# A hybrid decoder step: first two tiles by chunks, passage reordered with early clears, three query tiles from un-normalised sums

## The chip, the cores and the metric

One core of a Trainium2 chip runs one launch. The metric is the device time of the launch in microseconds (us); for several executions, the median. TensorE (PE) does the matmuls, VectorE (DVE), ScalarE (ACT) and GpSimd (POOL) the elementwise work, and SyncE (SP) issues most DMAs.

## What is computed

288 tokens of width 1024 (a prompt of 256 and eight samples of 4) go through one decoder layer:

```python
z = x @ w_in                                  # queries, keys, values, gates of two mixers
o_A = stick_breaking(...)                     # 8 heads x 64; the samples have 256 cached rows each
o_B = g0*compressed + g1*selected + g2*window # 8 heads, 2 groups, masked softmax with ALiBi
m = concat(rms(o_A) * g_A, rms(o_B) * g_B) @ w_out
h = (a - mean(a)) * rsqrt(var(a) + eps) * g + b      # a = alpha * x + m
q = h @ w_q                                   # 8 heads x 2 x 128
s = q . sub_keys; top-16 of each half, top-16 of the 16 x 16 sums -> 16 experts and weights a head
y = LayerNorm(alpha * h + sum weight * gelu(u_e . h) * v_e)
```

All is float32; keys, values and windows are returned too.

## The kernel before

**Tiles.** A weight tile is 128 x 1024 (512 KB). SP loads it into one of four ring slots; ACT rounds it to `w_hi` (L1225), DVE subtracts to get `w_lo` (L1606, issued in turn by `low_next`). An operand x is split in the same way. `project` (L650 to L652) then makes hi.hi, hi.lo and lo.hi for eight 128-column blocks into one PSUM bank: 24 products a tile.

**Stages.** 22 tiles of w_in (evacuated by ACT, counted by `z_sb`), the gates, the attention passage, 8 tiles of w_out, LayerNorm, 16 tiles of w_q with `pair_scores` after each pair of query tiles, then 128 tiles of the expert table u with routing on DVE, and 128 of v.

**Start.** SP loads w_in tile 0 in halves and x in quarters, ACT and SP share the x loads. 13 idle products (L674) run meanwhile. DVE forms `x_lo` (L1640) for each of eight blocks; tile 1 follows tile 0.

**Passage.** Each engine has its order written out by hand. PE: stick-breaking sums and the compression of the caches, then the samples' scores: 32 products with the cached keys `ks` (L782) and 8 with the new keys (L785) for each of two halves, each half released by eight `ks` page loads (`k_in`); ss_qk is raised at their end. Then values of the prompt (L722), transposes (L793, `ss_t`), `ns_scores` on selected and window keys (L802, L804), `ckT` (L820), compressed values (L828), compressed scores of samples (L834) and prompt (L842), `np_scores` (L858, L861), the samples' reverse sums (L924 to L928, `ss_tri`), and eight units `np_turn` (L873) / `np_values` (L894) with `ns_values` (L947) at the end. DVE: `lss` (L1731), `spb` (L1738), `ssc`, `sc_`, `np_max(0)`, `np_max(1)` (L1792, L1793), `nc_scale` (L1766), `np_scale`. ACT: `np_exp` (L1337), logarithms (L1317).

**Queues.** SP: w_in, 16 `ks` pages of 256 KB (L451), winkv, two writes of kv_out, three w_out tiles behind `ss_tri`, then eight writes of zeros of 1 MB each into `g_dram` (L462, 512-byte rows, called clears), the other w_out tiles, w_q. POOL: 16 `nsk` loads of 128 KB (L563), the `vs` loads (L567, L573) and, ahead of the units, a memset of the zeros (L569).

**LayerNorm.** `residual` (L1899) adds m to alpha x; squares on ACT; sums over features by products with ones (L1024 to L1030). While mean and deviation are made, PE runs `filling(22)` (L1020). DVE subtracts the mean (`center`, L1932) and multiplies by g and the deviation (`stretch`, L1936); ACT adds b and rounds to `h_hi` (L1435); DVE makes `h_lo` (L1941). The first three query tiles are taken together by blocks (L1059 to L1072) as the rows of h come.

Of the kernel before, what the change touches and what calls it, by code (L numbers as in the profile page):

```python
# [24 lines left out]
D = 1024  # L25
# [3 lines left out]
NB = 8  # L29
TS = 4  # L30
T = TP + NB * TS
DT = TP
SLOTS = 32
# [101 lines left out]
def trunk(nc, xT, w_in, w_gate, w_out, w_q, keysT, uT, v, u_rows, w1, pe_cmp, w2, vecs, ln2_rows, cache_sb, cache_nsa,  # L135
# [3 lines left out]
    with ctx:  # L139
# [66 lines left out]
        spb = at("spb", [128, 2, 2, PAST + 32], o + VA * T)  # L206
# [7 lines left out]
        lrow = at("lrow", [128, T], o + 7 * T)  # L214
        o += ZT * T
# [36 lines left out]
        lss = at("lss", [128, 768], at_ring + 1536)  # L252
        sc_ = at("sc_", [128, 8, 2, 32], at_cmp + 4096)
# [15 lines left out]
        w_hi = [at(f"w_hi{q}", [128, D], where, F32R) for q, where in enumerate(E + P + [at_a + KD * T + 2560])]  # L269
        w_lo = [at(f"w_lo{q}", [128, D], where + D, F32R) for q, where in enumerate(E + P + [at_a + KD * T + 2560])]  # L270
# [6 lines left out]
        qT = at("qT", [128, 4, T], r0)  # L277
# [95 lines left out]
        rm_add, ln_s, ln_q, ln_mu, ln_mu2 = map(sem, ("rm_add", "ln_s", "ln_q", "ln_mu", "ln_mu2"))  # L373
# [58 lines left out]
        def _(sp):  # L432
# [6 lines left out]
            sp.dma_start(ring[:, 0, 0:512], w_in[0][:, 0:512]).then_inc(x_in[0], 16)  # L439
            sp.dma_start(ring[:, 0, 512:D], w_in[0][:, 512:D]).then_inc(full[0], 16)  # L440
            for q in range(2, 4):
                sp.dma_start(xTs[:, 2 * q:2 * q + 2, :], xT[:, 2 * q:2 * q + 2, :]).then_inc(x_in[q], 16)
            for n in range(1, N_IN):
# [95 lines left out]
        def _(pool):  # L539
# [7 lines left out]
            pool.dma_start(wg[:, :, :], w_gate).then_inc(small_in, 16)  # L547
            nc.gpsimd.memset(qs_diag[:, :, :], 0.0)
# [20 lines left out]
            nc.gpsimd.memset(spread_out[:, :], 0.0)  # L569
# [68 lines left out]
        def _(pe):  # L638
# [34 lines left out]
            for _ in range(13):  # L673
                mm(ps[:, 7, :], idle_bits[:, 0:64].bitcast(BF16), idle_bits[:, :].bitcast(BF16), start=True, stop=True)  # L674

            x_parts, o_parts, h_parts = (x_hi, x_lo), (o_hi, o_lo), (h_hi, h_lo)
            with pe.Fori(0, 5) as i:
                for r in range(4):
                    pe.wait_ge(z_sb, 4 * i + r + 1)
                    project(r, x_parts, r, halves(i, r), x_low=None if r else x_l)  # L680
# [93 lines left out]

            pe.wait_ge(q_ready, 1)
# [21 lines left out]
            ins.then_inc(ss_t, 1)  # L797

            def ns_scores(br, keys_of):
# [3 lines left out]
                for w in range(2):  # L803
                    mm(ps[:, (3, 0)[br] + w, PAST:PAST + 32], qbd_b[:, 4 * w:4 * w + 4, :],  # L804
                       zT[:, (SK, WK)[br], TP:T], start=True, stop=True)
# [3 lines left out]
            ns_scores(0, lambda b: nsk[:, 2 * b:2 * b + 2, 0:128])  # L809
            for w in range(2):  # L810
                mm(ps[:, 3, 320 + w * 24:344 + w * 24], k("selrow", 32)[:, w * 128:(w + 1) * 128], gnat[0:32, 2, :],
                   start=True, stop=True)
            pe.wait_ge(win_in, 16)
            pe.wait_ge(ss_new, 1)
            ns_scores(1, lambda b: winkv[:, b, 0:PAST])

            hd = hdn[:, :, :].rearrange("p j (s g n) -> p j s g n", g=2, n=NC_)
            pe.wait_ge(ch_sb, 1)
            for g in range(2):
# [1565 lines left out]
```

## Time and profile before

| | us |
|---|---|
| three runs | 1017.07, 1020.25, 1020.06 |
| their median | 1020.06 |
| the profiled execution | 1017.82 |
| its span, first to last instruction | 1016.1 |
| PE busy in the span | 1005.5 |
| DVE busy | 825.8 |
| ACT busy | 547.3 |
| POOL busy | 363.1 |

The page gives shares over the whole span; the change touches the first 14 us, 65 to 170 us and 195 to 220 us, so those are read as timelines. A timeline row shows when an instruction (or a run of like ones, xcount) starts, how long it lasts, and in brackets how long its engine had been idle and what released it. The products of PE are pipelined: a row's time may overlap the next.

### The profile page before, as it was taken

Reading aid. Unit: us, or ns where it says so; the run is one execution under the profiler, and the core shown is the slowest. Engines: PE = TensorE matmul, PEld = TensorE weight load, DVE = VectorE, ACT = ScalarE, POOL = GpSimd, SP = SyncE. Lnnn points to the kernel's source line nnn. Section 1 sums busy time; section 2 is a strip of 40 time slices with the busy share of each in tenths; the row PEclk is TensorE's granted clock in tenths of the full one; section 3 lists DMA queues with packets and bytes.
Section 4 is the critical chain, followed back from the end, with each engine's and each line's share of the span. In section 5 each row is a group of like instructions: output and inputs, shape, how many; then the busy total and the mean of one; then the engine's idle time right before and its main releaser. Section 6 shows DMA issues by size and latency. Waiting matters only on the chain.

```text
span 1016.1 us, 21539 instructions
## 1 busy us (share of the span) xinstructions
PE 1005.5 (99%) x6603; PEld 891.5 (88%) x6603; DVE 825.8 (81%) x1834; ACT 547.3 (54%) x1040; POOL 363.1 (36%) x274
## 2 busy tenths in 40 slices
PE   9999999999999999999999999999999999999997
PEld 7997748999999999998888999988888888888875
DVE  5346577777899897889998699888888889999887
ACT  5436576553545444455556655455555555555553
POOL 0242300000088888888887884011111111111000
PEclk9999999999999999999999999999999999999999
DMA  8758889444588999998999967778888999899763
GB/s 286 261 213 273 277 282 315 151 134 143 189 217 206 240 334 308 318 346 269 277 262 293 236 133 191 246 251 276 311 297 301 310 322 319 306 306 300 261 219 124
DMA packets 124880, 261.75 MB, mean 258 GB/s; under 512 B 29168, under 2 KB 70144, under 8 KB 123520
## 3 DMA queue, kind: packets, MB, share of 16 engines
q1 hardware_dynamic: 91728, 204.60, 60.0%
q0 software_dynamic: 32816, 56.01, 20.7%
q10 hardware_dynamic: 288, 0.59, 0.2%
q8 instruction: 20, 0.33, 0.1%
q14 instruction: 28, 0.23, 0.1%
HBM read 236.83 MB, written 26.38 MB: 259 GB/s over the span
## 4 chain that ended last, share of the span: by engine, by line
PE 96%; DVE 2%; ACT 1%; DMA 0%; issue 0%; DVEq 0%; SPq 0%; ACTq 0%
PE ps L650 12%; PE ps L651 12%; PE ps L652 12%; PE ps L1168 11%; PE ps L1169 11%; PE ps L1170 11%; PE ps L1113 8%; PE ps L1115 4%; PE ps L1145 3%; PE ps L742 2%; PE ps L1039 1%; PE ps L894 1%; PE ps L873 1%; PE ps L861 1%; DVE w_lo L1606 1%; DMA ring<-in_w_in_dram 0%
## 5 line engine op out<-in xcount | busy, mean ns | idle before, releaser
L1606 DVE TENSOR_TENSOR w_lo<-ring,w_hi 128x512 fp32r<-128x512 f32 (+1 forms) x440 | 384.5, 878 | 109.1 <-ACT w_hi L1225 91.4
L1225 ACT CAST w_hi<-ring 128x512 fp32r<-128x512 f32 (+1 forms) x437 | 338.1, 774 | 75.1 <-PE ps L1170 54.4
L587 POOL DMA_INDIRECT gates<-spread_out,spread_at x128 | 241.8, 1889 | 128.7 <-DVE spread_out L2067 82.3
L650 PE MATMUL ps<-h_both,w_hi 128*128 128x256 f32 (+1 forms) x776 | 225.3, 290 | 0.3 <-issue 0.3
L651 PE MATMUL ps<-h_both,w_hi 128*128 128x256 f32 (+1 forms) x776 | 221.2, 285 | 0.0
L652 PE MATMUL ps<-h_both,w_lo 128*128 128x256 f32 (+1 forms) x776 | 220.1, 284 | 0.0
L1168 PE MATMUL ps<-w_hi,y_hi 128*128 128x512 f32 x496 | 193.2, 390 | 0.0
L1169 PE MATMUL ps<-w_hi,y_lo 128*128 128x512 f32 x496 | 193.0, 389 | 0.0
L1170 PE MATMUL ps<-w_lo,y_hi 128*128 128x512 f32 x496 | 193.0, 389 | 0.0
L650 PEld LDWEIGHTS ps<-h_both,w_hi 128*128 128x128 f32 x776 | 147.6, 190 | 1.3 <-issue 1.3
L651 PEld LDWEIGHTS ps<-h_both,w_hi 128*128 128x128 f32 x776 | 147.2, 190 | 0.0
L652 PEld LDWEIGHTS ps<-h_both,w_lo 128*128 128x128 f32 x776 | 145.8, 188 | 0.0
L1113 PE MATMUL ps<-h_both,w_hi 128*128 128x512 f32 x352 | 122.7, 392 | 0.0
L613 POOL DMA_INDIRECT vrow<-in_v_dram,expert x32 | 35.8, 1118 | 216.3 <-DVE sacc L2177 194.1
L1168 PEld LDWEIGHTS ps<-w_hi,y_hi 128*128 128x128 f32 x496 | 93.1, 188 | 20.5 <-DVE y_lo L2152 0.8
L1170 PEld LDWEIGHTS ps<-w_lo,y_hi 128*128 128x128 f32 x496 | 93.1, 188 | 19.3
L1169 PEld LDWEIGHTS ps<-w_hi,y_lo 128*128 128x128 f32 x496 | 93.1, 188 | 19.2
L1477 ACT ACTIVATE u_out<-ps 128x256 f32<-128x256 f32 x96 | 36.9, 385 | 119.6 <-PE ps L652 64.4
L1115 PE MATMUL ps<-h_both,w_lo 128*128 128x256 f32 x352 | 98.9, 281 | 0.0
L1113 PEld LDWEIGHTS ps<-h_both,w_hi 128*128 128x128 f32 x352 | 66.0, 188 | 14.7
L1550 ACT CAST y_hi<-a_in 128x256 fp32r<-128x256 f32 x92 | 37.5, 407 | 67.0 <-PE ps L1170 67.0
L1115 PEld LDWEIGHTS ps<-h_both,w_lo 128*128 128x128 f32 x352 | 66.4, 189 | 0.0
(404 smaller groups left out, 1482.9 us busy)
## 6 DMA issues: line engine op xcount, KB each, us to landing
ring<-in_uT_dram SPq DMA_DIRECT2D x128, 512.0 KB
ring<-in_v_dram SPq DMA_DIRECT2D x128, 512.0 KB
activations<-u_out SPq DMA_DIRECT2D x96, 128.0 KB
a_in<-activations SPq DMA_DIRECT2D x96, 128.0 KB, 4.2
ring<-in_w_in_dram SPq DMA_DIRECT2D x21, 512.0 KB
gates<-spread_out SPq DMA_DIRECT2D x8, 1024.0 KB, 9.1
ring<-in_w_q_dram SPq DMA_DIRECT2D x16, 512.0 KB
ks<-in_cache_sb_dram SPq DMA_DIRECT2D x16, 256.0 KB, 3.7
```

The costliest lines, as they stand in the source:

```text
L587: nc.gpsimd.indirect_dma_start(g_dram, bass.IndirectOffsetOnAxis(ap=spread_at[:, m:m + 1], axis=0), spread_out[:, m:m + 1], None, compute_ ...
L650: mm(out, hi, hi_, start=start, stop=False)
L651: mm(out, hi, lo_, start=False, stop=False)
L652: return mm(out, lo, hi_, start=False, stop=stop)
L1113: mm(ps[:, bank, :].rearrange("p (a t) -> p a t", a=2), w_hi[slot][:, block_], h_both[:, :, kd * T:kd * T + DT], start=kd == 0, stop=False)
L1115: ins = mm(ps[:, bank, DT:2 * DT], w_lo[slot][:, block_], h_hi[:, kd, 0:DT], start=False, stop=kd == KD - 1)
L1168: mm(out, hi, w_hi[slot][:, x], start=False, stop=False, skip_group_check=True)
L1169: mm(out, lo, w_hi[slot][:, x], start=False, stop=False, skip_group_check=True)
L1170: return mm(out, hi, w_lo[slot][:, x], start=False, stop=stop, skip_group_check=True)
L1225: nc.scalar.copy(w_hi[slot][:, x], ring[:, ring_slot, x]).then_inc(part_hi, 2 if half is None else 1)
L1550: nc.scalar.copy(y_hi[:, r % 2, :], a).then_inc(y_h, 1)
L1606: V.tensor_tensor(w_lo[slot][:, x], ring[:, ring_slot, x], w_hi[slot][:, x].bitcast(F32), ALU.subtract).then_inc(part_lo[ring_slot], 2 if ...
```

## The change

**Start.** Tiles 0 and 1 and x are loaded together, by 128 columns at first, then by 256 and 512. ACT and DVE split them chunk by chunk (`w_both`, `x_hi`, `x_lo`; DVE makes the first `x_hi`), and PE alternates between the two tiles for each chunk. Five idle products fewer.

**Passage.** The eight clears go ahead of the `ks` loads on SP; they wait for the zeros (set earlier on POOL) and for `z_sb` of tile 17. The compressed keys are made right behind the samples' scores, the prompt's compressed scores behind `ss_t`, the compressed values last. Products of 128 columns for four samples at once are made as four of 32 for the samples' new keys and values. The samples' reverse sums take `lss` split in high and low parts (fp32r). DVE takes the compressed scores first, `np_max(1)` goes behind `np_scale(0)`, and the wait for kv_out behind `nc_scale`. `spb` lies elsewhere.

**Query tiles.** For the first three, PE multiplies w_q with g * a (a not normalised, split as `xg_hi`, `xg_lo`), with two more columns that carry g and b (TX = 290). From the sums P, q = (P - mean * (w.g)) * deviation + w.b: DVE does the first two steps (`early_out`, two operations a tile), ACT adds w.b. `filling` is gone. Tiles 3, 4 and 5 follow by blocks; the first pair of scores comes behind tile 5, and `qT` has two buffers.

```diff
+            first_two(0, 1, x_in[0])
+            first_two(1, 1, k_in[0])
+            first_two(2, 2, x_in[1])
+            sp.dma_start(xTs[:, 4:6, :], xT[:, 4:6, :]).then_inc(x_in[2], 16)
+            first_two(4, 4, x_in[2])
+            sp.dma_start(xTs[:, 6:8, :], xT[:, 6:8, :]).then_inc(x_in[3], 16)
+            for n in range(2):
+                sp.sem_inc(full[n], 16)
...
+            sp.wait_ge(zero_done, 2)
+            sp.wait_ge(z_sb, 4 + N_IN - 4)
+            for q in range(8):
+                sp.dma_start(g_rows[:, 16 * q:16 * (q + 1), :],
+                             spread_out[:, :].unsqueeze(1).to_broadcast([128, 16, 128])).then_inc(cleared, 16)
             sp.wait_ge(pt_in, 16)
             sp.wait_ge(w_mm, 2 * N_IN)
             for n in range(PAGES):
...
-            sp.wait_ge(cmp_clear, 1)
-            for q in range(8):
-                sp.dma_start(g_rows[:, 16 * q:16 * (q + 1), :],
-                             spread_out[:, :].unsqueeze(1).to_broadcast([128, 16, 128])).then_inc(cleared, 16)
             sp.wait_ge(ss_pv, 2)
...
-            for _ in range(13):
+            for _ in range(8):
                 mm(ps[:, 7, :], idle_bits[:, 0:64].bitcast(BF16), idle_bits[:, :].bitcast(BF16), start=True, stop=True)
 
             x_parts, o_parts, h_parts = (x_hi, x_lo), (o_hi, o_lo), (h_hi, h_lo)
-            with pe.Fori(0, 5) as i:
+            pe.wait_ge(x_l, 1)
+            for kd in range(KD):
+                at_kd = slice(kd * 128, (kd + 1) * 128)
+                pe.wait_ge(x_h, (2, 3, 5, 6, 8, 9, 11, 12)[kd])
+                for n in range(2):
+                    mm(ps[:, n, 0:T], w_hi[n][:, at_kd], x_hi[:, kd, :], start=kd == 0, stop=False)
+                pe.wait_ge(x_l, (2, 4, 6, 6, 9, 9, 12, 12)[kd])
+                for n in range(2):
+                    mm(ps[:, n, 0:T], w_lo[n][:, at_kd], x_hi[:, kd, :], start=False, stop=False)
+                pe.wait_ge(x_l, (3, 5, 7, 8, 10, 11, 13, 14)[kd])
+                for n in range(2):
+                    ins = mm(ps[:, n, 0:T], w_hi[n][:, at_kd], x_lo[:, kd, :], start=False, stop=kd == KD - 1)
+                    if kd == KD - 1:
+                        ins.then_inc(w_mm, 2)
...
-                pe.wait_ge(k_in[w], 16 * 8)
+                pe.wait_ge(k_in[w], 16 * 8 + (32 if w == 0 else 0))
                 for hp in range(4):
                     for b in range(4 * w, 4 * w + 4):
                         mm(ps[b % 4 * 32:b % 4 * 32 + 32, w, 0:PAST], qs[:, hp, 32 * b:32 * b + 32],
                            ks[:, 2 * b:2 * b + 2, hp * 128:(hp + 1) * 128], start=hp == 0, stop=hp == 3)
                 for hp in range(4):
-                    ins = mm(ps[:, w, PAST:PAST + 32], qs[:, hp, 128 * w:128 * w + 128], zT[:, KA + hp, TP:T],
-                             start=hp == 0, stop=hp == 3)
+                    for b in range(4 * w, 4 * w + 4):
+                        ins = mm(ps[b % 4 * 32:b % 4 * 32 + 32, w, PAST:PAST + 32], qs[:, hp, 32 * b:32 * b + 32],
+                                 zT[:, KA + hp, TP:T], start=hp == 0, stop=hp == 3)
             ins.then_inc(ss_qk, 1)
+            block_keys()
...
+            prompt_blocks()
...
-            ns_scores(0, lambda b: nsk[:, 2 * b:2 * b + 2, 0:128])
             for w in range(2):
...
+            ns_scores(0, lambda b: nsk[:, 2 * b:2 * b + 2, 0:128])
...
+            block_values()
...
+            for x in (lss_hi, lss_lo):
+                mm(ps[:, 7, 0:512], neg[:, 0, :], x[:, 0:512], start=x is lss_hi, stop=False)
+            for x in (lss_hi, lss_lo):
+                mm(ps[:, 7, 0:256], neg[:, 1, :], x[:, 256:512], start=False, stop=False)
+            for x in (lss_hi, lss_lo):
+                mm(ps[:, 7, :].rearrange("p (a q) -> p a q", a=2), neg[new, 1, :],
+                   x[new, 512:768].unsqueeze(1).to_broadcast([32, 2, 256]), start=False, stop=x is lss_lo)
+            for x in (lss_hi, lss_lo):
+                ins = mm(ps[new, 6, 256:512], neg[new, 0, new], x[new, 512:768], start=x is lss_hi, stop=x is lss_lo)
+            ins.then_inc(ss_tri, 1)
...
+                        for b in range(4 * w, 4 * w + 4):
+                            mm(ps[b % 4 * 32:b % 4 * 32 + 32, w, 0:128], ptns[:, br, b * 32:(b + 1) * 32],
+                               vnat[0:32, 2, 4 + br, :], start=br == 0, stop=False)
...
+            def early_highs(c, at):
+
+                slot = (AT_Q + c) % 4
+                for m in at:
+                    kd = OUT_ORDER[m]
+                    pe.wait_ge(x_l, 14 + m + 1)
+                    block_ = w_hi[slot][:, kd * 128:(kd + 1) * 128]
+                    mm(ps[:, c, 0:TX], block_, xg_hi[:, kd, :], start=m == 0, stop=False)
+                    mm(ps[:, c, 0:TX], block_, xg_lo[:, kd, :], start=False, stop=False)
+
+            def early_lows(c):
+
+                slot, lows = (AT_Q + c) % 4, halves(0, AT_Q + c)
+                pe.wait_ge(lows[0], lows[2])
+                for kd in range(KD):
+                    ins = mm(ps[:, c, 0:TX], w_lo[slot][:, kd * 128:(kd + 1) * 128], xg_hi[:, kd, :],
+                             start=False, stop=kd == KD - 1)
+                ins.then_inc(w_mm, 2)
+
+            pe.wait_ge(m_pre, 5)
+            pe.wait_ge(part_hi, 2 * (AT_Q + 1))
+            early_highs(0, range(0, 3))
             pe.wait_ge(ln_s, 1)
             mm(ps[:, 4, 0:T], k("ones"), sum2[:, 0, :], start=True, stop=False)
-            pe.wait_ge(ln_q, 1)
+            pe.wait_ge(ln_s, 2)
             mm(ps[:, 5, 0:T], k("ones"), squ2[:, 0, :], start=True, stop=False)
             pe.wait_ge(m_pre, 8)
             mm(ps[:, 4, 0:T], k("ones"), xTs[:, 7, :], start=False, stop=True).then_inc(ln_mm, 1)
             pe.wait_ge(ln_sq, 8)
             mm(ps[:, 5, 0:T], k("ones"), sqb[:, 7, :], start=False, stop=True).then_inc(ln_v, 1)
-            filling(22)
+            early_highs(0, range(3, KD))
+            early_lows(0)
+            for c in range(1, EARLY):
+                pe.wait_ge(part_hi, 2 * (AT_Q + c + 1))
+                early_highs(c, range(KD))
+                early_lows(c)
...
+            pe.wait_ge(part_hi, 2 * (AT_Q + 4))
+            high_blocks(3, range(KD), h_hi, h_h, True)
+            pe.wait_ge(part_hi, 2 * (AT_Q + 5))
+            high_blocks(4, range(KD), h_hi, h_h, True)
             for kd in range(KD):
...
+                for m in (3, 4):
+                    high_blocks(m, (kd,), h_lo, h_l)
+            low_blocks(3)
+            low_blocks(4)
+            pe.wait_ge(part_hi, 2 * (AT_Q + 6))
+            high_blocks(5, range(KD), h_hi, h_h, True)
+            high_blocks(5, range(KD), h_lo, h_l)
+            low_blocks(5)
             pe.wait_ge(keys_in, 16)
+            behind = {0: (6,), 2: ()}
...
+            def weighted_high(c):
+                A(xg_hi[:, c, 0:T], xTs[:, c, :], ACT.Identity, scale=vec[:, 1, c:c + 1]).then_inc(x_h, 1)
...
+            for m in range(EARLY):
+                act.wait_ge(w_mm, 2 * (AT_Q + m + 1))
+                nc.scalar.copy(gb[:, m, :], ps[:, m, T:TX]).then_inc(q_gb, 1)
+                if m >= 1:
+                    high_of(AT_Q + m + 4)
...
+            dve.wait_ge(ss_ln, 1)
+            ss_parts = ((slice(0, 128), slice(0, 512)), (slice(0, 32), slice(512, 768)))
+            for rows, c in ss_parts:
+                ins = V.scalar_tensor_tensor(lss[rows, c], zss[rows, c], 0.0, lss[rows, c], ALU.max, ALU.add)
+            link(ins)
+            for rows, c in ss_parts:
+                ins = V.tensor_copy(lss_hi[rows, c], lss[rows, c])
+            link(ins)
+            for rows, c in ss_parts:
+                ins = V.tensor_tensor(lss_lo[rows, c], lss[rows, c], lss_hi[rows, c].bitcast(F32), ALU.subtract)
+            ins.then_inc(ss_sp, 1)
+
+            dve.wait_ge(ns_qk, 2)
...
             np_max(0)
-            np_max(1)
             nc_scale()
+            dve.wait_ge(out_kv, 32)
...
             np_scale(0)
+            np_max(1)
             ss_argument()
...
+            def weighted_low(m):
+                c = OUT_ORDER[m]
+                dve.wait_ge(x_h, 12 + m + 1)
+                V.scalar_tensor_tensor(xg_lo[:, c, 0:T], xTs[:, c, :], vec[:, 1, c:c + 1], xg_hi[:, c, 0:T].bitcast(F32),
+                                       ALU.mult, ALU.subtract).then_inc(x_l, 1)
...
+            def early_out(m):
+                dve.wait_ge(q_gb, m + 1)
+                link(V.scalar_tensor_tensor(qT(m), mean[:, :], gb[:, m, 0:1], ps[:, m, 0:T], ALU.mult, ALU.subtract))
+                V.scalar_tensor_tensor(qT(m), qT(m), -1.0, lrow[:, :], ALU.mult, ALU.mult).then_inc(q_raw, 1)
+
+            early_out(0)
+            early_out(1)
+            low_next()
+            early_out(2)
```

## Rows read from the trace of the kernel before

**Rows 1.** page, part 1 (busy us, share, instructions) and part 4 (chain)

```profile
PE 1005.5 (99%) x6603; PEld 891.5 (88%) x6603; DVE 825.8 (81%) x1834; ACT 547.3 (54%) x1040; POOL 363.1 (36%) x274
...
PE 96%; DVE 2%; ACT 1%; DMA 0%; issue 0%; DVEq 0%; SPq 0%; ACTq 0%
```

**Rows 2.** timeline of the start: start us, us, engine, line, operation, count, [idle before]

```profile
1.25 4.67 PE L674 MATMUL ps<-idle_bits 128*128 128x512 bf16 x13 [1.25 <-POOL idle_bits L540]
...
10.34 1.05 ACT L1225 CAST w_hi<-ring 128x1024 fp32r<-128x1024 f32 x1 [0.20 <-DMA ring<-in_w_in_dram]
...
11.51 3.75 DVE L1606 TENSOR_TENSOR w_lo<-ring,w_hi 128x1024 fp32r<-128x1024 f32 x3 [0.36 <-ACT w_hi L1225]
...
13.96 0.30 PE L650 MATMUL ps<-x_hi,w_hi 128*128 128x288 f32 x1
```

**Rows 3.** timeline of PE in the passage

```profile
108.43 1.08 PE L785 MATMUL ps<-zT,qs_flat 128*128 128x32 f32 x8
...
109.44 1.93 PE L782 MATMUL ps<-ks,qs_flat 128*32 128x256 f32 x32
...
112.31 1.52 PE L722 MATMUL ps<-zb,vnat 128*64 128x256 f32 x16
...
120.28 0.33 PE L834 MATMUL ps<-ckT,qbd_b 128*32 128x15 f32 x14
...
131.84 0.84 PE L873 MATMUL ps<-con,pb 128*128 128x128 f32 x6
...
154.98 1.52 PE L873 MATMUL ps<-con,pb 128*128 128x128 f32 x6
...
162.78 0.71 PE L947 MATMUL ps<-vnat,ptns 32*128 32x128 f32 x4
```

**Rows 4.** timeline of DVE in the passage

```profile
118.63 0.69 DVE L1731 SCALAR_TENSOR_TENSOR lss<-zss,lss 128x512 f32<-128x512 f32 x1 [3.53 <-ACT lss L1317]
...
120.71 0.76 DVE L1738 TENSOR_TENSOR spb<-ps,con 128x576 f32<-128x576 f32 x1 [1.07 <-PE ps L834]
...
125.12 0.42 DVE L1792 TENSOR_REDUCE sm<-ps 128x2 f32<-128x256 f32 x1 [0.27 <-PE ps L861]
125.46 0.68 DVE L1793 TENSOR_REDUCE sm<-ps 128x2 f32<-128x512 f32 x1
```

**Rows 5.** timeline of ACT, POOL and SP ahead of the sample scores

```profile
65.36 0.41 ACT L1251 ACTIVATE zT<-ps 128x288 f32<-128x288 f32 x1 [1.85 <-PE ps L652]
...
71.00 0.60 POOL L563 DMA_DIRECT2D nsk<-in_cache_nsa_dram  x1 [1.21 <-issue]
...
79.18 17.23 SPq L451 DMA_DIRECT2D ks<-in_cache_sb_dram  x16
...
88.37 0.54 POOL L563 DMA_DIRECT2D nsk<-in_cache_nsa_dram  x1 [0.60 <-issue]
```

**Rows 6.** line L462 with its time to landing; below it L451's landing

```profile
L462 SPq DMA_DIRECT2D gates<-spread_out x8: 697/2953/14203, 130.2 to 160.1; - x8
...
DMA to landing us min/median/max: 8.9/9.1/20.1
...
DMA to landing us min/median/max: 3.1/3.7/5.1
```

**Rows 7.** windows: us, PE, PEld, DVE, ACT, POOL busy; PEclk, DMA share, GB/s

```profile
142.00:144.00 2.00, 2.00 (x17) 0.99 (x19) 1.25 (x6) 2.00 (x11) 0.00 (x0) 1.00 0.57 204
...
155.00:155.50 0.50, 0.50 (x4) 0.50 (x5) 0.50 (x2) 0.50 (x5) 0.00 (x0) 0.50 1.15 347
```

**Rows 8.** timeline of PE and DVE behind LayerNorm's sums

```profile
197.20 3.27 PE L1020 MATMUL ps<-o_hi 128*128 128x288 f32 x22
...
208.22 1.80 DVE L1941 SCALAR_TENSOR_TENSOR h_both<-xTs,vec,h_both 128x288 fp32r<-128x288 f32 x4
...
219.23 1.05 PE L1039 MATMUL ps<-keys,qT 128*128 128x128 f32 x8
...
220.57 0.40 PE L650 MATMUL ps<-h_both,w_hi 128*128 128x288 f32 x1
```

More of the change, by code:

```diff
@@ L32 @@
 DT = TP
+TX = T + 2
+EARLY = 3
 SLOTS = 32
@@ L276, in trunk, with qT, q_bank @@
         r0 = at_e + 8 * D
-        qT = at("qT", [128, 4, T], r0)
+        qT_of = [at(f"qT{q}", [128, 4, T], where) for q, where in enumerate((r0, at_a + NE * DT - 3008))]
+        gb = at("gb", [128, EARLY, 2], rest)
+        def qT(m):
+            return qT_of[m // 4 % 2][:, m % 4, :]
+        def q_bank(m):
+            return {4: 6, 5: 7}.get(m, m % 4)
         r1 = r0 + 4 * T
@@ L437, in load, with first_two @@
                 sp.dma_start(ring[:, n % 4, :], src).then_inc(full[n % 4], 16)
[L439 to L443, printed above, removed]
+            def first_two(c, n, done):
+                x = slice(c * 128, (c + n) * 128)
+                sp.dma_start(ring[:, 0:2, x], w_in[0:2].rearrange("n p c -> p n c")[:, :, x]).then_inc(done, 16)
+            first_two(0, 1, x_in[0])
[6 more added lines that the diff above has]
+                sp.sem_inc(full[n], 16)
+            for n in range(2, N_IN):
                 load(n, w_in[n])
@@ L812, in _ @@
                    start=True, stop=True)
+            for b in range(NB):
+                mm(ps[b % 4 * 32:b % 4 * 32 + 32, 3, 288 + b // 4 * 16:288 + b // 4 * 16 + NC_], qbd_b[:, b, :],
+                   ckT[:, 1 + b, :], start=True, stop=True)
+            ns_scores(0, lambda b: nsk[:, 2 * b:2 * b + 2, 0:128])
             pe.wait_ge(win_in, 16)
@@ L1046, in sample_scores @@
                     rows = slice(q % 4 * 32, q % 4 * 32 + 32)
[L1047 removed]
+                    ins = mm(ps[rows, 7, 256:384], qT(q)[:, TP:T], keys[:, q, :], start=True, stop=True)
                 ins.then_inc(s_mm, 1)
[L1050 to L1061 removed]
@@ L1062, in _ @@
-            for kd in range(KD):
-                pe.wait_ge(h_l, kd + 1)
-                for c in range(3):
-                    ins = mm(ps[:, c, 0:T], w_hi[(AT_Q + c) % 4][:, kd * 128:(kd + 1) * 128], h_lo[:, kd, :],
-                             start=False, stop=c < 2 and kd == KD - 1)
-                    if c < 2 and kd == KD - 1:
-                        ins.then_inc(w_mm, 2)
-            lows = halves(0, AT_Q + 2)
-            pe.wait_ge(lows[0], lows[2])
-            for kd in range(KD):
-                ins = mm(ps[:, 2, 0:T], w_lo[(AT_Q + 2) % 4][:, kd * 128:(kd + 1) * 128], h_hi[:, kd, :],
-                         start=False, stop=kd == KD - 1)
@@ L1074, in _, with high_blocks, low_blocks @@
-            ins.then_inc(w_mm, 2)
+            def high_blocks(m, kds, x, ready, start=False):
+                for kd in kds:
+                    pe.wait_ge(ready, kd + 1)
+                    mm(ps[:, q_bank(m), 0:T], w_hi[(AT_Q + m) % 4][:, kd * 128:(kd + 1) * 128], x[:, kd, :],
+                       start=start and kd == 0, stop=False)
+            def low_blocks(m):
+                lows = halves(0, AT_Q + m)
+                pe.wait_ge(lows[0], lows[2])
+                for kd in range(KD):
+                    ins = mm(ps[:, q_bank(m), 0:T], w_lo[(AT_Q + m) % 4][:, kd * 128:(kd + 1) * 128], h_hi[:, kd, :],
+                             start=False, stop=kd == KD - 1)
+                ins.then_inc(w_mm, 2)
@@ L1079, in _ @@
                     sample_scores(c + 1)
-                for m in (c + 3, c + 4):
+                for m in behind.get(c, (c + 3, c + 4)):
                     if m < N_Q:
@@ L1926, in _ @@
             dve.wait_ge(ln_sq, 7)
-            into(squ2[:, 0, :], sqb[:, 6, :]).then_inc(ln_q, 1)
+            into(squ2[:, 0, :], sqb[:, 6, :]).then_inc(ln_s, 1)
             residual(7)
-            low_next()
+            for m in range(5, KD):
+                weighted_low(m)
             def center(c):
```

284 lines of the change are left out of this document (161 added, 123 removed).

## The prediction

> **What bounds the kernel now.** I read the page's busy times and its chain first: TensorE (PE) is busy 99% of the span and holds 96% of the chain [rows 1]. Both shares flatter it, since products that wait for an operand in their pipeline, and filling ones, count as busy. So I read the stretches that the change touches by start times: the timeline of all engines to 14 us, PE and VectorE (DVE) from 106 to 132, the sync engine's (SP's) DMA issues from 60 to 175, PE and DVE from 195 to 221. In the first, tile 2 starts late [rows 2]; in the second, PE is spread by short operations that wait on DVE and ScalarE (ACT) [rows 3, 4]; in the last, PE fills and then follows the normalised rows [rows 8]. Everything behind 221 us is steady and the change leaves it alone. The executed profile took 1017.82 us (span 1016.1), 2.2 below the median of 1020.06 and inside the three times; I make the sum against the profile and add the 2.2 back.
>
> **Part 1, the first two tiles by chunks.** Tile 2 starts at 13.96 [rows 2]; from there on the w_in tiles follow one another, so the gain is what that start moves. PE has the 48 products of two tiles ahead of it. Interleaving the tiles by 128 columns lets products start on 128 KB instead of 256 KB, but tile 2 stays behind the same bytes: ACT waits for its DMA 0.20 us now, and takes 1.05 from 10.34; the DVE half took 3.75 for three, 1.25 each [rows 2]. ACT's own new queue ends at about 10.7 by the same operations (four double casts and seven x casts). So 10.7 + 1.05 = 11.75, + 1.25 = 13.0, + 0.1 for the start: 13.1, a gain of 0.8. If DMA lands later than by today's order, 0.2; if the DVE half is used by halves, 1.2. The idle products fall from 13 to 8: they ended at 1.25 + 4.67 = 5.92 [rows 2] and will end near 4.7, 1 us more of idle PE ahead of the first product. I take that at nothing; the cover is that the products behind it are limited by landings. If the granted clock were lower for them, the 48 would take longer and eat the gain: I bound the part at -1.2 to +1.0.
>
> **Part 2, the passage.** Products: the 128-wide sample products of the scores, eight in 1.01 us (108.43 to 109.44) become 32 with 32-wide weights. Nearest row: 14 of that kind in 0.33, 0.024 each [rows 3], so 0.75, 0.3 less; at the rate of the longer ones (32 in 1.93 us, 0.06 each) they would cost 1.9, 0.9 more. They are as narrow as the former, so -0.3 twice, -0.6. Behind ss_qk (all sample scores, end 112.31) up to the turn at 131.84 there are 19.53 us [rows 3]. That stretch is DVE's and ACT's: lss waits 3.53 us for ACT's logarithm, spb 1.07 for PE [rows 4]. Splitting lss adds a cast and a subtraction for each of its two parts, about 2 x (0.69 + 0.41) = 2.2 on that path; the block scores taken ahead of it remove the 1.07, and np_max(1) (0.42 + 0.68, [rows 4]) leaves the path: 2.2 - 1.07 - 1.1 = 0. The cheaper products of the sums are hidden by it. Ends: +2.2 if neither goes, -2.0 if neither added pair is on it; 0 is nearest to the rows. Later, ns_values' products (0.71 for four [rows 3]) become 32-wide: -0.3 (0 to -0.4).
>
> **The clears.** Eight writes of 1 MB move on SP from behind the passage's w_out loads to ahead of the 16 ks page loads. Each blocks SP by a median 2.953 us, 355 GB/s, and lands 9.1 us after its issue began [rows 6]; SP is thus free some 6.2 us ahead of the last landing. They now start when ACT's evacuation of tile 17 ends: 65.36 + 0.41 [rows 5], less the 0.8 of part 1, 65.0. DMA is idle there, but the 16 nsk loads (2.1 MB, POOL's queue, 71.00 to 88.9 [rows 5]) use the same stretch: (8.39 + 2.10) / 0.355 = 29.5, end 94.5, SP free at 88.3. Today ks starts at 79.18 and takes 17.23 for 16, 1.077 each [rows 5]. The first one waits behind a full queue like a clear (2.95), to 91.3; 15 more to 107.4; the last lands 3.7 later (3.1 to 5.1) [rows 6], at 111.1. PE wants that second half at 109.44 [rows 3] less 0.8 less 0.3 = 108.3. **A new wait of 2.8 us (2.2 to 4.2)** takes the place of a cover of about 9 us; PE stands at the second wait on k_in, and all of the passage stands behind it. The first half (eighth issue 98.8, landing 102.5) is in time. winkv and the two kv_out writes are queued behind ks and leave 11 us later than now; their readers are ns_scores(1), now several short blocks further back, and the out_kv wait, now behind nc_scale, so I take nothing. Where the clears stood, SP was held for eight such issues while nothing on PE waited for it: no gain there.
>
> The Trainium skill, "DMA: Bandwidth & Descriptors", section "Issuing engines are not separate DMA queues", says that transfers of all issuing engines run on the same 16 DMA engines and interleave; that speaks against this move, and would make the nsk loads and the clears lengthen each other, as the sum above has it; were they separate, the clears would end by 88.7 and ks would be in time (second case below). No row of before shows these two together.
>
> **Part 3, query tiles from g*x.** PE fills from 197.20 for 3.27, starts the tiles behind that, and with five tiles and one pair done reaches 219.23; a pair of scores takes 220.57 - 219.23 = 1.34 [rows 8]. Without any wait, six tiles of 3.2 from the end of the sums (197.4) would end at 216.6; that work is 3.2 - 1.34 = 1.86 more than what stands at 219.23 now, so at most 4.5 us are to be had. But DVE has to make h_lo for tiles 3 to 5: now its last four end at 208.22 + 1.80 = 210.0 [rows 8]. It gets eight products by g (0.45 each, like h_lo), of which about three fall behind the last residual, 1.3; and three w_lo splits (1.25 each) move ahead of h_lo: h_lo ends about 214. The sums end 0.7 later (198.1). The three early tiles hide 9.6 of this, the high products of two tiles 4.3; the rest, about 2 us, is idle PE: 198.1 + 19.2 + 2.1 = 219.4 with six tiles and no pair, against 219.23: 1.86 - 0.17, **gain 1.7** (0 if DVE is a split later, 2.5 if earlier). The pair is due behind tile 5 instead, with early_out (two operations a tile) by then done on DVE. The routing's lists start when they do now.
>
> **Sum.** -0.8 - 0.6 - 0.0 - 0.3 + 2.8 - 1.7 = -0.6: 1017.2 for the profile, **1019.5** for the median.
>
> **Rivals.**
> (a) ks is in time: the clears end by 91 us, or ks issues faster than behind a full queue. For: DMA has nothing else from 66 to 71, and the first clear of three goes out in 0.70 us [rows 6]. Against: bytes. 1019.5 - 2.8 = 1016.7.
> (b) As (a), and the low clock goes too. From 155.00 the granted clock is 0.50, the lower of its two levels [rows 7]: six products L873 there took 1.52 us against 0.84 at 131.84 [rows 3]; over that spell I count 1.7 us. If the shorter passage or the missing clears shift it away: 1015.0.
> (c) The new wait brings such a spell itself: 1019.5 + 1.7 = 1021.2. The Trainium skill, "TensorE: Matmul & The Clock Gate", section "What's actually happening", has the gate fall after idleness; the rows show the fall at 155 with PE listed busy, so they don't tell how long a wait must be.
> (d) The other side, slower: the clears drain slowly while another queue moves data. For: from 142 to 144, with clears queued, all traffic was 204 GB/s [rows 7], and one clear's issue took 14.2 us [rows 6]. Then from 71.0 to 88.9 the clears and nsk get 204 instead of 355: 2.13 MB by 71.0, 3.65 until 88.9, the other 4.71 at 355 to 102.2. ks lands 7.7 later, the wait is 10.5: 1027.2. It decides once the clears end after 98.1 (3.6 later than my sum). Against: what ran at 142 was another kind of traffic, and a median of 2.953 says that this was the exception.
> (e) Part 3 doesn't do what it says: DVE, not the sums, sets when the query tiles run, and the gain is 0 (1021.2), or DVE's lateness stays for some tiles more (up to 1023.5).
>
> **How the numbers follow.** Forecast 0.42 (wait of 2.2 to 4.2, the other bounds around it: 1016.9 to 1021.5); (a) 0.22, (b) 0.10, (c) 0.08, (d) 0.13, (e) 0.05. About 0.3% (3.06 us) is what a measurement of this kernel can tell from no change: faster is below 1017.0, slower above 1023.1. Faster: (a), (b) and 0.03 of the forecast, 0.35; slower: (d) and 0.02 of (e), 0.15; same 0.50. The range of 1014.5 to 1024.5 takes in all but (d) and the lower end of (b), 0.17 together.
>
> **What would show it.** Right: tile 2 of w_in starts near 13.1; the last clear lands near 94.5 and SP's 16th ks issue ends near 107.4; PE's second set of ks products is released by the ks DMA near 111; the stretch from ss_qk's end to np_turn(1) still takes 19.5; filling is gone and the first three query tiles follow the sums without a gap, with a pause of 2 us at h_lo; tile 5 ends 24 to 25 us behind the end of the out tiles. Wrong: ks products released by ACT or nothing (a); SP issues of clears well over 3 us between 71 and 89 (d); DVE's splits rather than ks in PE's waits (e); or that 19.5 turning into 21.7 or 17.5, where I had set the parts against each other.

## The result

The changed kernel takes 1022.99 us (median of 8 runs, 1021.95 to 1026.07); the kernel before takes 1017.97 over the 8 runs that stand beside them. The ratio of the two is 1.0053 (95% interval 1.0044 to 1.0063): slower by 5.4 us by the ratio and 5.0 by the medians, where I had forecast 0.6 less and given slower a chance of 0.15. The profiled execution has a span of 1021.0 us, 4.9 more than before.

PE's waits of the changed kernel (us in total, times, longest):

```profile
PE ps L861 <- DMA ks<-in_cache_sb_dram: 7.0, 1, 7.0
PE ps L917 <- ACT pb L1444: 1.6, 1, 1.6
```

The first line is new, and larger than the whole loss. (The second is new too; it lies in a stretch that the table below gives as unchanged.) The first one's place, in PE's timeline of the changed kernel (start us, us, engine, line, operation, [idle before <-releaser]):

```profile
107.34 1.93 PE L861 MATMUL ps<-ks,qs_flat 128*32 128x256 f32 x32
109.09 0.48 PE L865 MATMUL ps<-zT,qs_flat 128*32 128x32 f32 x32
116.53 3.64 PE L861 MATMUL ps<-ks,qs_flat 128*32 128x256 f32 x32 [6.96 <-DMA ks<-in_cache_sb_dram]
...
120.52 0.68 PE L840 MATMUL ps<-hdn,w2s 128*64 128x135 f32 x4
...
140.05 0.88 PE L932 MATMUL ps<-con,pb 128*128 128x128 f32 x6
```

The second set of ks products waits for its load, and then takes 3.64 us instead of the 1.93 of the first set: the windows of that stretch (PEclk stands third from the right) show the granted clock at 0.50, the lower of its two levels. I call a stretch at that level a spell.

```profile
114.00:116.00 2.00, 0.00 (x0) 0.00 (x0) 0.00 (x0) 0.00 (x0) 1.06 (x2) 0.55 0.98 344
116.00:118.00 2.00, 1.47 (x16) 0.78 (x20) 0.00 (x0) 0.00 (x0) 1.10 (x5) 0.50 1.08 457
```

SP's queue shows why the load is late (first: the clears, second: ks):

```profile
66.62 23.63 SPq L479 DMA_DIRECT2D gates<-spread_out  x8
91.33 19.66 SPq L485 DMA_DIRECT2D ks<-in_cache_sb_dram  x16
111.03 0.45 SPq L487 DMA_DIRECT2D winkv<-in_win_kv_dram  x1
```

ks starts at 91.33, where it had started at 79.18 [rows 5].

**Where the time went**, by the same points of both traces. The starts of before that stand in no [rows] are from its timeline:

| from, to | before | after | difference |
|---|---|---|---|
| start to the gates' products | 78.05 | 78.82 | +0.77 |
| to the first ks products | 28.52 | 28.52 | 0 |
| to the end of the samples' scores | 5.74 | 13.18 | +7.44 |
| to the second unit's turn | 19.53 | 19.53 | 0 |
| to the first w_out product | 35.93 | 34.27 | -1.66 |
| to LayerNorm's sums | 27.63 | 28.47 | +0.84 |
| to the scores of tiles 10 and 11 | 54.08 | 51.90 | -2.18 |

The differences add up to 5.2; 0.3 comes back behind the last row. Of the 7.44, 6.96 is the wait and 1.71 the low clock in the second set (3.64 - 1.93); the rest, -1.23, is the narrower products. The -1.66 is no gain of the change: it is the spell of 1.71 that the trace of before has at 155 [rows 7] and this one doesn't; with the old order and no spell there, this stretch takes 34.33 in three traces further down (query tiles alone and the two of the start alone). The last two rows go together, since six early products (0.80) now stand ahead of the sums: w_out is as long as before, and the query part is 1.38 shorter.

**The start.** Three rows of the start of the changed kernel: ACT's wait for the last w_in chunks, DVE's split of tiles 2 and 3, and tile 2, which began at 13.96 [rows 2] and now begins at 14.66.

```profile
9.55 0.62 ACT L1332 CAST w_both<-ring 128x512 fp32r<-128x512 f32 x1 [1.68 <-DMA ring<-in_w_in_dram]
...
13.29 2.36 DVE L1733 TENSOR_TENSOR w_lo<-ring,w_hi 128x1024 fp32r<-128x1024 f32 x2 [0.32 <-DVE x_lo L1765]
...
14.66 0.37 PE L680 MATMUL ps<-x_hi,w_hi 128*128 128x288 f32 x1 [0.42 <-ACT zT L1360]
```

The last row names ACT, but that product also waits for the first of DVE's two splits (half of 2.36, from 13.29 to about 14.5). In the last kernel of this document, with this start, the same row names the split:

```profile
14.03 0.37 PE L683 MATMUL ps<-x_hi,w_hi 128*128 128x288 f32 x1 [0.59 <-DVE w_lo L1736]
```

**The query tiles.** DVE's h_lo ends at 216.91 + 3.52 = 220.4, PE waits 0.67 for its first row, and with six tiles and no pair it is at 226.18 (before: five tiles and a pair at 219.23 [rows 8]).

```profile
216.91 3.52 DVE L2109 SCALAR_TENSOR_TENSOR h_both<-xTs,vec,h_both 128x288 fp32r<-128x288 f32 x8
...
217.48 0.40 PE L1142 MATMUL ps<-h_both,w_both 128*128 128x288 f32 x1 [0.67 <-DVE h_both L2109]
...
226.18 1.05 PE L1127 MATMUL ps<-keys,qT 128*128 128x128 f32 x8
```

### The profile page after: what moved, and what is told of

It is laid out like the page before. It is cut to its first block, busy times and chain, and to the rows that moved or that the text cites. A ratio compares the mean times of both kernels' runs of the same rounds, so it can differ in the third digit from the quotient of the medians.

```text
span 1021.0 us, 21698 instructions
## 1 busy us (share of the span) xinstructions
PE 999.6 (98%) x6670; PEld 886.2 (87%) x6670; DVE 833.7 (82%) x1855; ACT 550.6 (54%) x1052; POOL 357.2 (35%) x274
## 4 chain that ended last, share of the span: by engine, by line
PE 88%; DVE 4%; SPq 4%; ACT 1%; DMA 1%; issue 1%; DVEq 0%; ACTq 0%
PE ps L1261 11%; PE ps L1262 11%; PE ps L1263 11%; PE ps L680 11%; PE ps L681 11%; PE ps L682 11%; PE ps L1206 8%; PE ps L1208 4%; PE ps L1238 3%; SPq L479 2%; SPq L485 1%; PE ps L1127 1%; SPq L484 1%; DMA ring<-in_w_in_dram 1%; DMA ks<-in_cache_sb_dram 1%
## 5 line engine op out<-in xcount | busy, mean ns | idle before, releaser
L1733 DVE TENSOR_TENSOR w_lo<-ring,w_hi 128x512 fp32r<-128x512 f32 (+1 forms) x358 | 286.7, 805 | 61.4 <-ACT w_hi L1318 51.1
L1318 ACT CAST w_hi<-ring 128x512 fp32r<-128x512 f32 (+1 forms) x356 | 254.7, 716 | 71.2 <-PE ps L1263 53.3
L617 POOL DMA_INDIRECT gates<-spread_out,spread_at x128 | 235.3, 1838 | 130.1 <-DVE spread_out L2247 83.1
L1733 DVE TENSOR_TENSOR w_both<-ring,w_both 128x1024 fp32r<-128x1024 f32 x78 | 95.4, 1225 | 39.6 <-ACT w_both L1318 37.8
L680 PE MATMUL ps<-h_both,w_hi 128*128 128x256 f32 (+1 forms) x432 | 127.4, 295 | 0.3 <-issue 0.3
L681 PE MATMUL ps<-h_both,w_hi 128*128 128x256 f32 (+1 forms) x432 | 122.8, 284 | 0.0
L682 PE MATMUL ps<-h_both,w_lo 128*128 128x256 f32 (+1 forms) x432 | 122.1, 283 | 0.0
L1262 PEld LDWEIGHTS ps<-w_hi,y_lo 128*128 128x128 f32 x496 | 93.1, 188 | 19.1
L681 PE MATMUL ps<-h_both,w_both 128*128 128x256 f32 (+1 forms) x320 | 91.2, 285 | 0.0
L682 PE MATMUL ps<-h_both,w_both 128*128 128x256 f32 (+1 forms) x320 | 90.7, 284 | 0.0
L680 PE MATMUL ps<-h_both,w_both 128*128 128x256 f32 (+1 forms) x320 | 90.6, 283 | 0.1
L680 PEld LDWEIGHTS ps<-h_both,w_hi 128*128 128x128 f32 x432 | 82.3, 190 | 1.1 <-issue 1.1
L1318 ACT CAST w_both<-ring 128x1024 fp32r<-128x1024 f32 x78 | 81.5, 1046 | 2.5 <-DMA ring<-in_w_in_dram 2.5
L681 PEld LDWEIGHTS ps<-h_both,w_hi 128*128 128x128 f32 x432 | 82.1, 190 | 0.0
L682 PEld LDWEIGHTS ps<-h_both,w_lo 128*128 128x128 f32 x432 | 81.1, 188 | 0.0
```

The lines of the kernel that those rows point to most:

```text
L617: nc.gpsimd.indirect_dma_start(g_dram, bass.IndirectOffsetOnAxis(ap=spread_at[:, m:m + 1], axis=0), spread_out[:, m:m + 1], None, compute_ ...
L680: mm(out, hi, hi_, start=start, stop=False)
L681: mm(out, hi, lo_, start=False, stop=False)
L682: return mm(out, lo, hi_, start=False, stop=stop)
L1262: mm(out, lo, w_hi[slot][:, x], start=False, stop=False, skip_group_check=True)
L1318: nc.scalar.copy(w_hi[slot][:, x], ring[:, ring_slot, x]).then_inc(part_hi, 2 if half is None else 1)
```

## The experiments

Theory A: the clears ahead of ks hold SP, so ks is issued late; all of the loss is there, and the other two structures change little. Theory B: the reordered passage is slower by itself. Theory C: it is not the queue but the 16 DMA engines that the clears share with other transfers. All medians of this part stand beside runs of the kernel before on the same chip: 1017.36 for the four kernels that undo one part, 1017.21 for the clears, the query tiles and the passage alone and for the split clears with the old start, 1018.02 for the other four.

### Undoing one part of the change

**Clears back.** The eight clears go behind the three w_out loads again:

```diff
-            sp.wait_ge(zero_done, 2)
-            sp.wait_ge(z_sb, 4 + N_IN - 4)
-            for q in range(8): ...            # ahead of ks
...
+            sp.wait_ge(zero_done, 2)
+            for q in range(8): ...            # behind w_out tiles 0, 1, 3
             sp.wait_ge(ss_pv, 2)
```

> The changed kernel with the eight clears back behind the three w_out loads; all else as changed. Theory A (the clears hold SP, so the ks loads land late; the wait of 6.96 us and the slow second set of ks products are theirs): no wait of PE on ks, second set of ks products in 1.9 us instead of 3.6, from the first ks products to the second prompt unit 24.6 us instead of 32.7; 1023.0 falls by 8.1 to 1014.9, or to 1016.6 if the low clock at 155 us of the kernel before comes back. Theory B (the reordered passage itself is slower): it stays above 1019. Theory C (DMA engines shared with the vs loads, not SP's queue): a wait of 2 us or more on ks stays.

1016.0, ratio 0.9986 (0.9975 to 0.9996): 7 us of the changed kernel's time are gone by this edit. No wait on ks; from the first ks products to the second unit 24.79 us, with a spell inside (116 to 119). Theory B falls. But a wait comes that neither of the two traces had, in the w_out tiles (waits of PE, the kernel with the clears back):

```profile
PE ps L679 <- DVE w_both L1732: 1.3, 1, 1.3
```

Its SP queue, and that of the kernel before, differ little: the last five w_out loads go out behind the clears, at 162.62 and at 163.14.

```profile
127.17 35.36 SPq L491 DMA_DIRECT2D gates<-spread_out  x8
162.62 10.65 SPq L458 DMA_DIRECT2D ring<-in_w_out_dram  x5
```

What differs is PE: its w_out products start at 165.80 instead of 167.77. The late clears were just early enough for PE as it came there in the trace of before, with its spell at 155; the kernels with one part alone, below, show what happens without it.

**Start back** (all of the change's edits to the first two tiles reversed, all else as changed):

```diff
-            first_two(0, 1, x_in[0])
...
+            sp.dma_start(ring[:, 0, 0:512], w_in[0][:, 0:512]).then_inc(x_in[0], 16)
...
-            for _ in range(8):
+            for _ in range(13):
```

> The changed kernel with the old start (two tiles one after the other, 13 idle products). Theory A (the chunks make tile 2 start 0.7 later, since the last chunks of two tiles land together): tile 2 starts at 14.0 instead of 14.66, everything up to the clears 0.8 earlier, the ks wait unchanged at 7.0; 1022.2. Rival: the start is hidden by the clears (their start follows another event): no change, 1023.0. Rival: the chunks gain, as I had forecast, and 14.66 is an accident of one execution: slower, 1023.8.

1022.54, ratio 1.0051 (1.0037 to 1.0065). The gates' products start at 77.96 instead of 78.82 and the clears 0.86 earlier, yet the second set of ks products only 0.08 earlier (116.45), so PE waits 7.67 instead of 6.96: what the start gives, the ks loads take. In this trace the clock is low from 111 to 121, three spells' worth.

**Both back**, by the two edits above: the passage's order and the query tiles remain.

> The changed kernel with the old start and with the clears back behind the three w_out loads: passage order and query tiles alone remain. Theory A: the sum of the two, 1014.1 (1015.8 with a low clock spell in the passage), faster than the kernel before by 2 to 4 us: 1.5 from the query tiles, 0.6 from the narrow products, and the spell. Theory B (the reordered passage is slower): 1018 or more.

1016.01, ratio 0.9986 (0.9974 to 0.9999). From the first ks products to the second unit 23.56 us against 25.27, without a spell; and the wait in the w_out tiles is 2.06, the larger since PE gets there at 164.35.

**No gate**: the wait for tile 17 goes, and the clears follow the last w_in load.

```diff
             sp.wait_ge(zero_done, 2)
-            sp.wait_ge(z_sb, 4 + N_IN - 4)
             for q in range(8): ...
```

> The changed kernel without the clears' wait for tile 17 of w_in: they are queued right behind the last w_in load, some 10 us earlier. Theory A (it is the time at which the clears end that counts): SP is free near 82, the ks loads start 8 us earlier, the wait on ks falls from 7.0 to 0 to 1 and the slow second set goes; 1014.5 to 1016. Theory C (contention): the w_in loads or page loads slow down, PE waits ahead of 79 us, and less than half of the 8 us is won: above 1019.

1015.97, ratio 0.9997 (0.9980 to 1.0014). The wait on ks falls from 7.0 to 0.5, and winkv, queued behind ks, adds one of 0.7. SP's queue:

```profile
87.10 19.43 SPq L484 DMA_DIRECT2D ks<-in_cache_sb_dram  x16
```

The expected 82 was too early: the clears began 10.2 us earlier (56.46) but took 29.57 us instead of 23.63, so SP was free only 4.2 us earlier. There they met w_in and page loads, which in the changed kernel already move 384 GB/s from 50 to 60 us (first line), no less than all traffic moves while the clears run there (345 and 364, the other two):

```profile
50.00:60.00 10.00, 10.00 (x77) 10.00 (x76) 3.68 (x3) 4.42 (x7) 4.61 (x9) 1.00 1.00 384
...
70.00:75.00 5.00, 5.00 (x40) 5.00 (x38) 2.53 (x9) 0.41 (x1) 1.68 (x3) 1.00 1.15 345
...
80.00:85.00 5.00, 4.79 (x43) 4.12 (x44) 2.58 (x8) 4.19 (x9) 1.61 (x3) 1.00 1.12 364
```

Theory C has that part. But the wait fell by 6.5, more than the 4.2 by which ks moved: the last issue ends at 106.53 and PE goes on at 109.63, 3.1 later; in the changed kernel it was 5.5 later (110.99, 116.53). There POOL's vs loads had begun:

```profile
108.63 0.54 POOL L598 DMA_DIRECT2D vs<-in_cache_sb_dram  x1 [12.17 <-issue]
```

That is the timeline of the changed kernel; the times from issue to landing of its last four ks loads (line L485 by windows, two in the first) grow from 3.2 to 5.8 as the vs loads set in:

```profile
DMA to landing us min/median/max: 3.2/3.4/3.6
...
DMA to landing us min/median/max: 4.6/4.6/4.6
...
DMA to landing us min/median/max: 5.8/5.8/5.8
```

Without the gate the last three take 2.8 to 3.4. Between those two crowds ks looks bound by its issue, not by the engines: the issues come some 1.1 us apart, since SP loads a page number into a register for each, and from 102 to 104 the engines moved

```profile
102.00:104.00 2.00, 2.00 (x10) 1.60 (x9) 1.93 (x4) 0.26 (x1) 0.00 (x0) 1.00 0.74 246
```

246 GB/s at a share of 0.74 (a window of the changed kernel). So A and C both have a part: SP's queue sets when ks begins, and the gate's run shows that the clears hold it for longer in a crowd. That the vs loads lengthen the last landings is read from the times of these traces; no run moved the vs loads.

### One part alone on the kernel before

Each of these kernels is the kernel before with some edits of the change: the clears alone (their place on SP and the zeros' on POOL), the query tiles alone (all behind the out tiles), the passage alone (clears at their old place) and the start alone.

> The kernel before with the early clears alone (zeros set early, eight clears ahead of the ks loads, gated by tile 17). Theory A: the clears' own price, without the other parts: ks wait of about 7.5 (need 109.4, landing 0.8 earlier than in the changed kernel, as in the run with the old start), slow second set: 8 us up to the second prompt unit; the spell of low clock at 155 may go. 1017.4 + 7.5 + 0 to 1.7 = 1025 to 1026.6. Rival: in the slow order of before the clears' absence later gives some of it back: 1023.

1027.02, ratio 1.0092 (1.0069 to 1.0114): slower by 9.4 us. The wait on ks is 6.6, and the clock is low from 112 to 119 and again from 163 to 167. Nothing is given back later.

> The kernel before with the query tiles from un-normalised sums alone. Theory A: from the end of the out tiles to pair 10 the trace of the changed kernel is 1.4 to 1.5 us shorter in like work, whatever stands ahead of it: 1017.4 - 1.5 = 1015.9. Rival (the gain only stands because the passage ends at another phase): 1017.4.

1016.16, ratio 0.9990 (0.9979 to 1.0002): 1.05 us, not to be told from none by the interval. The trace bears the mechanism out: from the sums to the scores of tiles 10 and 11 51.88 us, against 54.08, less the 0.80 moved ahead of the sums: 1.40, as in the changed kernel (1.38).

> The kernel before with the reordered passage alone, clears at their old place (zeros set early). Theory A: from the first ks products to the second unit 23.6 us without a low-clock spell, against 25.3 (-1.7), but a wait on w_lo of 1.3 to 2.1 us in the w_out tiles takes most of it back, since the late clears hold SP while the last w_out loads are due: 1017.4 - 1.7 + 1.5 = 1017.2. Rival (that wait belongs to the new query part): no wait, 1015.7.

1017.27, ratio 1.0000 (0.9988 to 1.0011). 23.78 us from ks to the second unit (before 25.27), and 2.0 of waiting in the w_out tiles: what the new order gains, the late clears take. In this trace, as in that with both back, a spell begins within 1 us of the end of that wait.

> The kernel before with the first two tiles by chunks alone. Theory A (both tiles' last halves wait for one transfer of 512 KB, behind which 24 products and two more splits of tile 2 stand): the gate products start between 78.2 and 78.8 instead of about 78.0; 1017.4 + 0.5, not to be told from no change. Rival (as forecast, the chunks gain 0.8): gate products at 77.3, 1016.6.

1018.26, ratio 1.0002 (0.9992 to 1.0012). Tile 2 starts at 14.65, the gates' products at 78.81. The times can't tell it; over the traces, the gates' products start between 78.23 and 78.82 in the five with this start and between 77.79 and 78.19 in the seven with the old one: 0.54 later on the mean.

This trace shows something else. Its passage and its clears are those of the kernel before, but it has no spell in the passage, so PE reaches w_out at 166.99, ahead of the 167.77 of before in spite of the later start, and there it waits:

```profile
174.14 0.37 PE L662 MATMUL ps<-o_hi,w_both 128*128 128x288 f32 x1 [1.62 <-DVE w_both L1652]
```

ACT's cast ahead of that split waited 2.56 us for a w_out load; SP had sent the last five from 163.42 on, behind the clears. The two other kernels with the old order and no spell have the wait too: 0.57 with the query tiles alone, 1.09 with the next one. So the late clears cost the kernel before something as well, and the spell in its trace hid that.

The start alone again, with one transfer cut in two:

```diff
-            first_two(4, 4, x_in[2])
+            first_two(4, 2, x_in[2])
             sp.dma_start(xTs[:, 6:8, :], xT[:, 6:8, :]).then_inc(x_in[3], 16)
+            first_two(6, 2, x_in[3])
```

> As the run with the chunks alone, but the last four chunks of w_in come in two transfers, so that ACT begins at the first half. Theory A (the size of that transfer sets tile 2's start): ACT's cast of the fifth chunk pair starts 0.5 to 0.6 earlier, gate products 0.4 to 0.6 earlier than with the chunks alone. Rival (the DMA as a whole is late, by its 512-byte rows): no earlier start; the last chunk lands when it did.

1018.22, ratio 1.0005 (0.9996 to 1.0014). ACT's cast of the fifth pair starts at 9.44 instead of 9.54, tile 2 at 14.79: theory A's 0.5 is not there. With the same start in the last kernel below, it starts at 8.66 and tile 2 at 14.03. The landings vary by more than the edit, and why the chunks land late stays open.

### A version that beats both

**Half of the clears in either place.** First with one edit to the changed kernel:

```diff
             sp.wait_ge(z_sb, 4 + N_IN - 4)
-            for q in range(8): ...            # ahead of ks
+            for q in range(4): ...
...
                 load(AT_OUT + n, w_out[n])     # n in (0, 1, 3)
+            for q in range(4, 8): ...
             sp.wait_ge(ss_pv, 2)
```

> The changed kernel with one edit: only four of its early clears stay at their place, gated by tile 17; the other four go behind the three w_out loads. Theory A: SP is free at about 78 instead of 90, ks is issued from 79.5 on, no wait on ks and no slow second set: 1023.0 - 7 to -8.7 = 1014.3 to 1016. Rival (any clear ahead of ks costs by sharing the DMA engines): a wait of 2 to 4 us stays, 1018 to 1020.

1014.17, ratio 0.9963 (0.9949 to 0.9977). ks starts at 79.76, no wait on it, no wait in the w_out tiles. So four clears ahead of ks bring no wait, and eight bring one of seven microseconds. Then the same with the old start and without the gate (the edits shown above):

> The changed kernel with the old start, four clears behind the last w_in load without the wait for tile 17, the other four behind the three w_out loads. Theory A (late clears delay the w_out loads, early ones the ks loads; half of them fits in either place): no wait on ks, none above 0.3 on w_lo in the w_out tiles: 1016.0 (both parts back) - 1.5 to 2 = 1014 to 1014.5. Rival (the waits are contention on the DMA engines): one of the two waits stays above 1 us, 1015.5 to 1016.

1013.25, ratio 0.9962 (0.9947 to 0.9977): 3.9 us faster than the kernel before and, by the two ratios, 9 faster than the changed one. Its SP queue:

```profile
56.50 14.02 SPq L466 DMA_DIRECT2D gates<-spread_out  x4
79.19 17.33 SPq L472 DMA_DIRECT2D ks<-in_cache_sb_dram  x16
...
125.98 23.61 SPq L482 DMA_DIRECT2D gates<-spread_out  x4
149.69 20.02 SPq L454 DMA_DIRECT2D ring<-in_w_out_dram  x5
```

ks starts where it did before, and the last w_out loads 13 us earlier than before.

And with the cut transfer in place of the old start:

> The changed kernel with four clears behind the last w_in load (no gate), four behind the w_out loads, and its own start with the last four chunks in two transfers. If the transfer's size was what made the chunks late, this is as fast as the split clears with the old start or faster by up to 0.5: 1012.8 to 1013.3; if not, 0.5 slower: 1013.8.

1013.97, ratio 0.9963 (0.9950 to 0.9976): the start makes no difference that these runs show.

## Why the prediction was wrong

The mechanism was named, in its place: the second wait on k_in behind the clears. The step that failed is the size of that term, +2.8 in the sum and 6.96 in the trace, with the low clock behind the wait put at nothing; it turned the sign of the sum. The 1022.99 lies inside the range of 1014.5 to 1024.5, but this says little: the range held both directions and was laid around a median of 1020.06 of three runs, where eight runs gave 1017.97.

**The clears: 2.8 forecast, 6.96 measured, and 1.71 for the clock.** Four steps of that sum were each short. Their start was put at 65.0, with the 0.8 that the start would gain; it was 66.62 (+1.6). ks began 24.7 after the first clear instead of 23.3 (+1.4): the eight clears held SP for 23.63, close to the sum by bytes, though each issue took a median 3.450 instead of 2.953; the other 1.1 is the page number that SP loads ahead of the first ks issue, which the sum left out. The 16 issues took 19.66 instead of 19.1 (+0.6). The last landing was put at 3.7 by the row of the loads in an open field; with vs beside it, it was 5.5 (+1.8). Together 5.4; PE's need was 1.3 later than I had it, so the wait was 4.2 longer. My bounds of 2.2 to 4.2 came from the landing alone (3.1 to 5.1), and even that was passed; the other three had no bounds. I looked at what ks is queued behind, not at what it runs into when it is late. Rival (d), a drain at 204 GB/s, falls: the windows of the clears have 345 and 364, a clear's landing took at most 11.4 us, none the 20.1 of [rows 6], and the last one was in by 86.4 + 11.2 = 97.6, ahead of its 98.1. Its other sign, issues over 3 us, was there all the same, so that sign alone decided nothing.

**The clock.** Case (c), the wait that brings a spell with it, had 0.08; in these traces it came with every wait of this size. All three kernels with eight gated clears ahead of ks have the clock low in it, for 3.4 us of lost clock or more; of the eleven other traces none loses more than 1.71. In the changed kernel the granted clock fell to 0.50 at 114.2, 4.6 us into the wait, and the products behind it took 3.64 us for 1.93. Here the Trainium skill's "TensorE: Matmul & The Clock Gate", section "What's actually happening" (idleness brings the throttle back), agrees with the rows. How much of it is the wait's own is not shown: the same passage with no wait on ks, or one of 0.5, has a spell of 1.71 at 116 to 118 in three traces (clears back, no gate, half of the clears).

**The start: -0.8 forecast, +0.77.** Here the step that failed is the one behind "tile 2 stays behind the same bytes": I took ACT's queue from the operations' lengths and let none of them wait. ACT waited four times for a DMA, 0.39, 0.39, 0.99 and 1.68 us, 3.45 in all, and tile 2's split stood behind that. PE's first product came at 5.40 (before: 6.87), but PE then waited 0.35 and 0.88 for chunks inside the two tiles, where the old order had all of tile 0 to work on while tile 1 landed. Why the chunks landed late stays open.

**The passage: -0.6 and 0 and -0.3 forecast.** The samples' new-key products were mis-sized by their row: I took 0.024 each from L834, and at the upper clock 32 of them took 0.28 to 0.41 (from their start to that of the next products), so the samples' scores end after 4.16 us instead of 5.74 (kernel with split clears): -1.58. The 0 of the chain behind it was right (19.37 against 19.53 there). The -0.3 of ns_values was hardly there: units and values take 34.27 us against 34.33 in the old order without a spell.

**What I said the clears' old place costs: nothing.** It was not even true of the kernel before, only of its one trace: with the old order and no spell, PE meets the last w_out loads and waits 0.57 to 1.62 there. With the passage shorter, 1.3 to 2.1 us come back there. I priced the cover of the moved step where it went to, and not the cover of the place that it left, against the new times.

**The query tiles: -1.7 forecast, -1.38.** Right in kind: filling gone, h_lo the wait. Its first row made PE wait 0.67, and DVE's pace of one row in 0.43 us the rest, about where the 2 us had been put. Rival (e) falls.

## What to carry to other kernels

When a transfer is moved ahead of others in a queue, follow the delayed transfers to their last landing: what releases the first one, what the issuing engine does between issues, and what they run into once they are late. Four such terms, each short, made this wait more than twice its estimate. A buffer-clearing job of this size is better cut: half of it fitted into each of two gaps that the whole overflowed. And a gain of a microsecond ahead of a queue can be taken back by it, so the edit that shortens a stretch and the one that frees the queue behind it have to be tried together. One trace can hide a wait behind a spell of low clock: compare stretches with the clock at the same level.

## What the hardware showed that I had not expected

In these 14 traces the low-clock spells of TensorE cost equal portions. Summed over 100 to 182 us, the clock lost is 1.71 us in the trace of before, 3.41 after, 5.12 with the start back and with the clears alone, 1.71 in five others, and 0 in the remaining five. With no wait on ks of a microsecond or more they stand at various places (116 to 118, 155, 172), with PE listed as busy for all or most of them.

Lost clock also goes with the spread of one kernel's runs. Without the gate, the fastest of the 12 runs (1014.02 us) has a mean granted clock of 0.999 and the slowest (1022.63) 0.991: over their spans 1.0 and 9.2 us of lost clock, 8.2 apart, where the times are 8.6 apart. Over the 12 runs the lost clock and the time go together with a slope of 1.0 (correlation 0.96; the clock is recorded to 0.001, 1 us of a span). In the kernel before they hardly do (0.10 and 0.15 in two sets of 29 and 23 runs, 0.60 in a third of 24). That fits a wait that swallows clock lost ahead of it, as the late w_out loads make one, but no traces of fast and slow runs of it were compared.

Thirty-two products with 32-wide weights for four row groups take 0.41 us or less at the upper clock, where eight with 128-wide weights took 1.01 [rows 3].
